# Expert stage of a streaming encoder layer: a two-slot loop on three engines becomes 32 written-out slots

## The chip, the cores and the metric

The kernel runs on one core of one Trainium2 chip. The metric is device time in microseconds from launch to end. "TensorE" multiplies matrices, "VectorE" and "ScalarE" do elementwise work, "GpSimd" and "SyncE" here mostly issue DMAs. In profile rows they are PE (PEld for its weight loads), DVE, ACT, POOL and SP; a q behind a name (SPq, PEldq) is that engine's sequencer, which issues DMAs and does register work.

## The reference

One layer of a streaming encoder for 1024 prompt tokens, 16 meta tokens and 64 sample tokens: attention and a gated recurrence side by side, then a mixture of experts, of which this is the core:

```python
gates = (one_hot(g_idx) * within * g_top).reshape(-1, N_EXPERTS)   # top group, top 2 of its 4 experts
y = zeros(t.shape)
for e in range(N_EXPERTS):                                         # 16 experts
    he = silu(t @ w1[e]) * (t @ w3[e])                             # 1024 -> 256
    y = y + gates[:, e:e + 1] * (he @ w2[e])                       # 256 -> 1024
```

Every token goes to two experts, in fp32. The 1088 tokens of the two requests give 2176 pairs of token and expert.

## The kernel before, in words

The pairs are sorted by expert and padded to tiles of 128 rows. There are at most SLOT_TILES = 32 such tiles, called slots; an expert has one or more consecutive slots. A table `expert_of`, computed on the chip, gives each slot's expert. Slot s needs the expert's first weights (w1 and w3 side by side, 2 MB), its second weights (w2, 1 MB) and 128 gathered token rows.

To keep fp32 accuracy every operand is split in a high and a low part and every product is three matmuls (L1638, L1639, L1640). The raw weights have one buffer, `w13_in`, in four chunks; they are split again for each slot, also when the expert stays the same. The work of slot s:

- SyncE (`moe_loads`): per chunk, two weight DMAs with condition `new` (L1426), which move data only if slot s has another expert than slot s-1. Before chunk c it waits until VectorE has split chunk c of slot s-1 (`s_w13lo`). Then it waits for the finished rows of slot s-3 and stores them (L1440, L1430). The order is its program's: loads of s, store of s-3, loads of s+1. It reads the expert numbers from memory into registers (L1404, L1407).
- GpSimd (`moe_pool`, written out already): gathers tokens (L1474), makes the low part of w2 (L1514) and loads w2 (L1483), with the same condition.
- ScalarE (`moe_act`): high parts of the weights of slot s+1 in four chunks (L1539), of w2 in two halves (L1559), the SiLU of slot s (L1575), the high part of the turned tokens of slot s+1 (L1547), half of the result rows of slot s-1 (L1552), the high part of the gate product (L1588).
- VectorE (`moe_dve`): the low parts of the same (L1842 weights, L1852 turned tokens, L1900 gate product), the product with the SiLU (L1889), the other half of the result rows (L1857).
- TensorE (`moe_pe`): the first product of slot s (24 matmuls of 512 columns), eight transposes of slot s+1's tokens (L1649), the second product of slot s-1 (12 matmuls), two transposes of slot s's gate rows (L1696). That is 46 matmuls and 46 weight loads a slot, in this order, on every engine's program by hand.

The four engines other than GpSimd run `body(it, j, first, last)` through `expert_turns`: slots 0 to 3 written out, slots 4 to 27 in a hardware loop of 12 turns of two slots (`eng.Fori(2, turns - 1)`), slots 28 to 31 written out. In the loop the slot number `s = it * UN + j` is in a register, so each wait such as `wait_ge(s_mh, s)` compares with a register that has to be computed first; outside it is a constant.

Of the kernel before, what the change touches and what calls it, by code (L numbers as in the profile page):

```python
# [41 lines left out]
SLOT_TILES = (2 * sum(MOE_ROWS) - NE) // P + NE  # L42
# [60 lines left out]
def hybrid_layer(nc, x_prompt, x_sample, cache_ckv, cache_krope, state_hgrn, meta_tokens, attn_norm, w_in, q_norm,  # L103
# [1269 lines left out]
    UN = 2  # L1373
# [4 lines left out]
    def uses(j):  # L1378

        return len(range(j, SLOT_TILES, UN))  # L1380

    def expert_turns(eng, body):

        turns = SLOT_TILES // UN - 1
        assert SLOT_TILES % UN == 0
        for it in range(2):
            for j in range(UN):
                body(it, j, it == 0, False)
        with eng.Fori(2, turns - 1) as it:
            for j in range(UN):  # L1390
                body(it, j, False, False)
        for it in (turns - 1, turns):
            for j in range(UN):
                body(it, j, False, it == turns and j == UN - 1)

    def is_zero(s):
        return isinstance(s, int) and s == 0

    def chunk(w, c):
        return w[:, 2 * c:2 * c + 2, :]  # L1400
# [127 lines left out]
    def moe_act(act):  # L1528
        act.wait_ge(s_rexp, 1)
        act.activation(rt[:, 8, 0:45], rt[:, 8, 0:45], ACT.Exp).then_inc(s_rexp, 1)  # L1530

        def split_weights(s, j):

            for c in range(WC):
                act.wait_ge(s_w13in[c], 32 * (s + 1))

                if c == 0 and not (isinstance(s, int) and s < UN):
                    act.wait_ge(s_mh, s - UN + 1)
                act.activation(chunk(w13_hi[j], c), chunk(w13_in, c), ACT.Copy).then_inc(s_w13hi, 1)  # L1539

        def turned(s):

            act.wait_ge(s_mx, s + 1)
            if not is_zero(s):
                act.wait_ge(s_mh, s)
            for half in range(2):
                act.activation(xg_hi[:, 4 * half:4 * half + 4, :],  # L1547
                               ps[:, half, :].rearrange("p (a b) -> p a b", a=4), ACT.Copy).then_inc(s_mxa, 1)

        def y_half(s, j):  # L1550
            act.wait_ge(s_my, s + 1)
            return act.activation(y_row[:, j, 0:512], ps[:, 6, :], ACT.Copy).then_inc(s_mya, 1)  # L1552

        def split_second(s, j, c):

            if c == 0 and not (isinstance(s, int) and s < UN):
                act.wait_ge(s_my, s - UN + 1)
            act.wait_ge(s_w2in[c], 16 * (s + 1))
            act.activation(w2_hi[j][:, c], w2_in[:, c], ACT.Copy).then_inc(s_w2hi, 1)  # L1559

        split_weights(0, 0)
        turned(0)

        def body(it, j, first, last):
            s = it * UN + j
            start = first and j == 0
            if not last:
                split_weights(s + 1, (j + 1) % UN)
            split_second(s, j, 0)
            if last:  # L1570
                split_second(s, j, 1)
            act.wait_ge(s_mh, s + 1)
            if not start:
                act.wait_ge(s_mg, s)
            act.activation(act_h, ps[:, 3 + j, 0:FF], ACT.Silu).then_inc(s_ms, 1)  # L1575
            if not last:
                turned(s + 1)
                split_second(s, j, 1)
            if not start:

                if not first:
                    free_y(act, it, j)
                y_half(s - 1, (j - 1) % UN)

            act.wait_ge(s_mgt, s + 1)
            if not start:
                act.wait_ge(s_my, s)
            act.activation(g_hi, ps[:, 2, 0:2 * P].rearrange("p (a b) -> p a b", a=2),  # L1588
                           ACT.Copy).then_inc(s_mga, 1)

        expert_turns(act, body)
        free_last(act)
        y_half(SLOT_TILES - 1, (SLOT_TILES - 1) % UN)
        for t in range(NT):
            R = MOE_ROWS[t]
            act.wait_ge(s_comb, NT + t + 1)
            if t:
                act.wait_ge(s_ysq, t)
            act.activation(y_sq[0:R], res[t][0:R, :], ACT.Square,
                           accum_out=y_stat[0:R, 0, t:t + 1]).then_inc(s_ysq, 1)  # L1600
# [17 lines left out]
    def moe_pe(pe):  # L1618

        pe.wait_ge(s_cnt, 1)  # L1620
        pe.matmul(ps[:, 0, 0:NT * NE], tab[:, C_TRI:C_TRI + P], rt[:, 15, :], start=True, stop=True)
        pe.matmul(ps[:, 1, 0:NT * NE], ones, rt[:, 15, :], start=True, stop=True).then_inc(s_rank, 1)
        pe.matmul(ps[:, 3, 0:P], ones, tab[:, C_TRI:C_TRI + P], start=True, stop=True).then_inc(s_col, 1)
        for k in range(2):
            for t in range(NT):
                n = k * NT + t
                if t == 0:
                    pe.wait_ge(s_onehot, 3 + k)
                ins = pe.matmul(ps[:, 2, 0:2 * SLOT_TILES], pos_at[0:MOE_ROWS[t], n, :], tok_at[0:MOE_ROWS[t], n, :],
                                start=n == 0, stop=n == 2 * NT - 1)  # L1630
        ins.then_inc(s_tokt, 1)
        for n in range(WARM):
            pe.matmul(ps[:, 5, :], tab[:, C_ID:C_ID + P], tab[:, C_ID:C_ID + 512], start=True, stop=True)

        def product(out, parts, w, start, stop):

            (x_hi, x_lo), (w_hi, w_lo) = parts, w
            pe.matmul(out, x_hi, w_hi, start=start, stop=False)  # L1638
            pe.matmul(out, x_hi, w_lo, start=False, stop=False)  # L1639
            return pe.matmul(out, x_lo, w_hi, start=False, stop=stop)  # L1640

        def turn(s, it, j):

            pe.wait_ge(s_xg[j], 16 * (it + 1))
            if not is_zero(s):
                pe.wait_ge(s_mxa, 2 * s)
                pe.wait_ge(s_mxv, 2 * s)
            for kc in range(KC):
                ins = pe.transpose(ps[:, kc // 4, (kc % 4) * P:(kc % 4 + 1) * P], xg[:, j, kc * P:(kc + 1) * P], ident)  # L1649
            ins.then_inc(s_mx, 1)  # L1650

        def down(s, j):

            pe.wait_ge(s_mga, s + 1)
            pe.wait_ge(s_mgv, s + 1)
            pe.wait_ge(s_w2hi, 2 * s + 2)
            pe.wait_ge(s_w2lo, 2 * s + 2)
            if not is_zero(s):
                pe.wait_ge(s_mya, s)
                pe.wait_ge(s_myv, s)  # L1660
            for n in range(2):
                cols = slice(n * 512, (n + 1) * 512)
                for c in range(2):
                    ins = product(ps[:, 6 + n, :], (g_hi[:, c, :], g_lo[:, c, :]),
                                  (w2_hi[j][:, c, cols], w2_lo[j][:, c, cols]), c == 0, c == 1)
            ins.then_inc(s_my, 1)

        pe.wait_ge(s_toki, 1)
        turn(0, 0, 0)

        def body(it, j, first, last):
            s = it * UN + j
            start = first and j == 0

            if not first:
                pe.wait_ge(s_mg, s - UN + 1)
            for kc in range(KC):
                if kc % 4 == 0:
                    pe.wait_ge(s_mxa, 2 * s + kc // 4 + 1)
                    pe.wait_ge(s_mxv, 2 * s + kc // 4 + 1)  # L1680
                if kc % 2 == 0:
                    pe.wait_ge(s_w13hi, WC * s + kc // 2 + 1)
                    pe.wait_ge(s_w13lo, WC * s + kc // 2 + 1)
                ins = product(ps[:, 3 + j, :], (xg_hi[:, kc, :], xg_lo[:, kc, :]),
                              (w13_hi[j][:, kc, :], w13_lo[j][:, kc, :]), kc == 0, kc == KC - 1)
            ins.then_inc(s_mh, 1)
            if not last:
                turn(s + 1, it + (j + 1) // UN, (j + 1) % UN)
            if not start:
                down(s - 1, (j - 1) % UN)  # L1690
            pe.wait_ge(s_mg, s + 1)
            if not start:
                pe.wait_ge(s_mga, s)
                pe.wait_ge(s_mgv, s)
            for c in range(2):
                ins = pe.transpose(ps[:, 2, c * P:(c + 1) * P], g_row[:, c * P:(c + 1) * P], ident)  # L1696
            ins.then_inc(s_mgt, 1)

        expert_turns(pe, body)
        down(SLOT_TILES - 1, (SLOT_TILES - 1) % UN)  # L1700

    def moe_dve(dve, link):
# [198 lines left out]
                              g_hi.bitcast(F32),  # L1901
                              ALU.subtract).then_inc(s_mgv, 1)

        expert_turns(dve, body)
        first_adds(range(2))
        free_last(dve)
        y_half(SLOT_TILES - 1, (SLOT_TILES - 1) % UN)
# [166 lines left out]
    def _(act):  # L2074
# [67 lines left out]
        attention_act(act)  # L2142
        end_phase(act, 1)
        moe_act(act)

    @blk.tensor
# [152 lines left out]
```

## Time and profile before

| what | value |
|---|---|
| runs before, us | 1200.32, 1204.63, 1195.77; median 1200.32 |
| profiled execution, us | 1196.12 |
| its span, first to last instruction, us | 1194.2 |
| mean granted TensorE clock | 0.962 of full |
| first product of slot 0, of slot 4, of slot 28 | 830.84, 872.40, 1109.51 us from the span's start |

Profile times count from the span's start. The profiled execution is 4.2 us below the median of the runs. Rows of a timeline read: start us, duration us, engine, line, operation, output<-input, shape, count, and in brackets the engine's idle time before and who ended it.

### The profile page before, as it was taken

Reading aid. Unit: us, or ns where it says so; the run is one execution under the profiler, and the core shown is the slowest. Engines: PE = TensorE matmul, PEld = TensorE weight load, DVE = VectorE, ACT = ScalarE, POOL = GpSimd, SP = SyncE. Lnnn points to the kernel's source line nnn. Section 1 sums busy time; section 2 is a strip of 40 time slices with the busy share of each in tenths; the row PEclk is TensorE's granted clock in tenths of the full one; section 3 lists DMA queues with packets and bytes.
Section 4 is the critical chain, followed back from the end, with each engine's and each line's share of the span. In section 5 each row is a group of like instructions: output and inputs, shape, how many; then the busy total and the mean of one; then the engine's idle time right before and its main releaser. Section 6 shows DMA issues by size and latency. Waiting matters only on the chain.

```text
span 1194.2 us, 18236 instructions
## 1 busy us (share of the span) xinstructions
PE 1065.5 (89%) x5777; PEld 860.0 (72%) x5777; DVE 697.2 (58%) x1326; ACT 525.4 (44%) x1025; POOL 344.9 (29%) x368
## 2 busy tenths in 40 slices
PE   5999999998987899999999999975999999999940
PEld 4889889984555777777778777863777777777830
DVE  4330610118666667576575655448777777787867
ACT  4432421213532333323333333313787878788823
POOL 3100510000541111111110100201656565666655
PEclk9999999999989999899999999996999999999985
DMA  7340141122579586465555444834988687877667
GB/s 273 118 164 1 45 127 64 45 78 68 195 272 364 199 322 244 174 229 207 205 198 198 156 170 151 295 143 160 302 313 325 243 282 248 284 253 255 246 240 278
DMA packets 105764, 242.83 MB, mean 203 GB/s; under 512 B 15248, under 2 KB 63840, under 8 KB 95456
## 3 DMA queue, kind: packets, MB, share of 16 engines
q1 hardware_dynamic: 81312, 117.42, 28.8%
q0 software_dynamic: 23328, 122.17, 28.7%
q10 hardware_dynamic: 1056, 2.36, 0.6%
q8 instruction: 39, 0.64, 0.2%
q14 instruction: 29, 0.24, 0.1%
HBM read 243.31 MB, written 48.94 MB: 245 GB/s over the span
## 4 chain that ended last, share of the span: by engine, by line
PE 58%; DMA 12%; DVE 9%; issue 8%; ACT 5%; SPq 5%; POOL 2%; POOLq 0%; DVEq 0%; ACTq 0%
DMA below<-in_w 8%; PE ps L1076 5%; PE ps L2189 4%; PE ps L2191 4%; PE ps L2190 4%; PE ps L929 4%; PE ps L947 3%; SPq L1426 3%; PE ps L1117 3%; PE ps L1025 3%; PE ps L1118 3%; PE ps L2184 3%; PE ps L2183 3%; PE ps L2185 3%; PE ps L1121 3%
## 5 line engine op out<-in xcount | busy, mean ns | idle before, releaser
L1842 DVE TENSOR_TENSOR low<-below,high 128x1024 fp32r<-128x1024 f32 x128 | 156.6, 1260 | 35.3 <-ACT high L1539 31.8
L1638 PE MATMUL ps<-high 128*128 128x512 f32 x384 | 156.1, 407 | 10.8 <-DVE low L1852 7.2
L1514 POOL TENSOR_TENSOR low<-below,high 128x1024 fp32r<-128x1024 f32 x62 | 129.0, 2081 | 94.0 <-ACT high L1559 93.1
L1639 PE MATMUL ps<-low,high 128*128 128x512 f32 x384 | 150.7, 392 | 0.0
L1640 PE MATMUL ps<-high,low 128*128 128x512 f32 x384 | 150.6, 392 | 0.0
L1539 ACT ACTIVATE high<-below 128x1024 fp32r<-128x1024 f32 x128 | 130.3, 1070 | 38.6 <-DMA below<-in_w 37.9
L653 ACT ACTIVATE arena<-ps 128x512 f32<-128x512 f32 (+8 forms) x100 | 50.1, 511 | 172.0 <-PE ps L929 171.6
L929 PE MATMUL ps<-arena 128*128 128x128 f32 (+4 forms) x613 | 94.3, 277 | 7.5 <-ACT arena L653 2.2
L797 POOL DMA_DIRECT2D high<-wo_dram x34 | 18.7, 549 | 281.6 <-PE ps L1121 270.8
L1638 PEld LDWEIGHTS ps<-high 128*128 128x128 f32 x384 | 72.5, 189 | 28.1 <-issue 12.8
L947 PE MATMUL ps<-arena 128*128 128x64 f32 (+2 forms) x624 | 83.4, 269 | 6.9 <-DVE arena L702 2.9
L929 PEld LDWEIGHTS ps<-arena 128*128 128x128 f32 (+4 forms) x613 | 71.4, 148 | 25.0 <-issue 17.6
L2189 PE MATMUL ps<-high 128*128 128x512 f32 (+3 forms) x216 | 83.8, 388 | 3.7 <-DVE low L2231 3.7
L947 PEld LDWEIGHTS ps<-arena 128*128 128x128 f32 (+2 forms) x624 | 77.6, 191 | 11.2 <-DVE arena L700 3.9
L896 ACT ACTIVATE arena<-ps,arena 80x320 f32<-80x320 f32 (+8 forms) x72 | 51.5, 715 | 73.9 <-DVE arena L1291 45.4
L1640 PEld LDWEIGHTS ps<-high,low 128*128 128x128 f32 x384 | 72.4, 189 | 16.0
L1076 PE MATMUL ps<-arena 96*128 96x512 f32 (+3 forms) x192 | 79.1, 522 | 5.3 <-ACT arena L902 2.8
L2041 POOL TENSOR_SCALAR arena<-arena 128x1 f32<-128x1 f32 (+7 forms) x33 | 10.3, 312 | 251.4 <-ACT arena L878 94.2
L2191 PE MATMUL ps<-high,low 128*128 128x512 f32 (+3 forms) x216 | 82.8, 383 | 0.0
L2190 PE MATMUL ps<-low,high 128*128 128x512 f32 (+3 forms) x216 | 82.6, 382 | 0.0
L1639 PEld LDWEIGHTS ps<-low,high 128*128 128x128 f32 x384 | 72.7, 189 | 13.2
L1559 ACT ACTIVATE high<-below 128x1024 fp32r<-128x1024 f32 x64 | 67.8, 1060 | 22.8 <-DMA below<-in_w 22.5
(251 smaller groups left out, 2215.8 us busy)
## 6 DMA issues: line engine op xcount, KB each, us to landing
below<-in_w SPq DMA_DIRECT2D x256, 256.0 KB
high<-wo_dram POOLq DMA_DIRECT2D x36, 1024.0 KB, 5.9
low<-wo_dram POOLq DMA_DIRECT2D x36, 1024.0 KB, 8.6
below<-in_w POOLq DMA_DIRECT2D x64, 512.0 KB
y_dram<-arena SPq DMA_DIRECT2D x32, 512.0 KB
arena<-in_x_prompt SPq DMA_DIRECT2D x15, 512.0 KB
below<-in_w_in SPq DMA_DIRECT2D x14, 512.0 KB, 7.7
out<-arena SPq DMA_DIRECT2D x9, 512.0 KB, 2.7
```

Source lines behind the costliest of these rows:

```text
L929: ins = pe.transpose(ps[0:width, 4 + g % 2, n * P:n * P + rows], src, ident[0:rows, 0:rows])
L947: ins = pe.matmul(ps[0:R, 6, hd * VD:(hd + 1) * VD], p_t[0:w, ip % 2, n, 0:R], v_rows[0:w, kb, hd * VD:(hd + 1) * VD], start=hd == 0 and g ...
L1076: ins = pe.matmul(ps[0:R, bank + n // 512, 0:m], q_t[0:QD, hd, 0:R], k_t[0:QD, hd, k0 + n:k0 + n + m], start=True, stop=True)
L1514: pool.tensor_tensor(w2_lo[s % UN][:, c], w2_in[:, c], w2_hi[s % UN][:, c].bitcast(F32), ALU.subtract).then_inc(s_w2lo, 1)
L1539: act.activation(chunk(w13_hi[j], c), chunk(w13_in, c), ACT.Copy).then_inc(s_w13hi, 1)
L1638: pe.matmul(out, x_hi, w_hi, start=start, stop=False)
L1639: pe.matmul(out, x_hi, w_lo, start=False, stop=False)
L1640: return pe.matmul(out, x_lo, w_hi, start=False, stop=stop)
L1842: dve.tensor_tensor(chunk(w13_lo[j], c), chunk(w13_in, c), chunk(w13_hi[j], c).bitcast(F32), ALU.subtract).then_inc(s_w13lo, 1)
L2189: pe.matmul(out, x_hi[:, kc, toks], wh[:, kc, 0:nn], start=kc == 0, stop=False)
L2190: pe.matmul(out, x_hi[:, kc, toks], wl[:, kc, 0:nn], start=False, stop=False)
L2191: ins = pe.matmul(out, x_lo[:, kc, toks], wh[:, kc, 0:nn], start=False, stop=kc == KC - 1)
```

## The change

The loop goes on TensorE, ScalarE and VectorE. Each calls `expert_slots`, which calls the same `body` 32 times with Python integers, so 24 slots' instructions take the place of one loop body of two. Order and number of operations stay the same, the waits get constants. SyncE still calls `expert_turns`, and GpSimd is untouched.

```diff
@@ -1379,6 +1379,11 @@
+    def expert_slots(body):
+
+        for s in range(SLOT_TILES):
+            body(s // UN, s % UN, s < UN, s == SLOT_TILES - 1)
+
     def expert_turns(eng, body):
 
         turns = SLOT_TILES // UN - 1
@@ moe_act
-        expert_turns(act, body)
+        expert_slots(body)
         free_last(act)
@@ moe_pe
-        expert_turns(pe, body)
+        expert_slots(body)
         down(SLOT_TILES - 1, (SLOT_TILES - 1) % UN)
@@ moe_dve
-        expert_turns(dve, body)
+        expert_slots(body)
         first_adds(range(2))
```

## Rows read from the trace of the kernel before

In groups 2 and 9 the columns are: stretch, its us, then busy us and (x instructions) of PE, PEld, DVE, ACT and POOL, the granted clock, the DMA engines' busy share, GB/s.

**Rows 1.** The page, part 1: busy time of each engine.

```profile
PE 1065.5 (89%) x5777; PEld 860.0 (72%) x5777; DVE 697.2 (58%) x1326; ACT 525.4 (44%) x1025; POOL 344.9 (29%) x368
```

**Rows 2.** Busy time by stretch: slots 4 to 27, then slots 28 to 31.

```profile
872.40:1109.50 237.10, 228.94 (x1104) 185.88 (x1105) 183.90 (x217) 192.65 (x265) 147.01 (x122) 1.00 0.79 277
1109.50:1147.50 38.00, 36.78 (x179) 30.24 (x177) 27.12 (x35) 28.26 (x40) 24.52 (x23) 1.00 0.54 199
```

**Rows 3.** TensorE in order of time: around the starts of slots 28, 29, 7, 16, 3.

```profile
1109.51 0.48 PE L1638 MATMUL ps<-high 128*128 128x512 f32 x1
...
1118.74 0.38 PE L1696 MATMUL ps<-arena 128*128 128x128 f32 x2
1118.87 0.48 PE L1638 MATMUL ps<-high 128*128 128x512 f32 x1
...
901.34 0.38 PE L1696 MATMUL ps<-arena 128*128 128x128 f32 x2
902.22 0.47 PE L1638 MATMUL ps<-high 128*128 128x512 f32 x1 [0.50 <-DVE low L1852]
...
991.89 0.44 PE L1696 MATMUL ps<-arena 128*128 128x128 f32 x2 [0.36 <-DVE arena L1889]
992.93 0.47 PE L1638 MATMUL ps<-high 128*128 128x512 f32 x1 [0.61 <-DVE low L1852]
...
860.24 0.38 PE L1696 MATMUL ps<-arena 128*128 128x128 f32 x2
861.07 0.47 PE L1638 MATMUL ps<-high 128*128 128x512 f32 x1 [0.46 <-ACT high L1547]
```

**Rows 4.** TensorE's waits over slots 4 to 27: total us, times, longest us.

```profile
PE ps L1638 <- DVE low L1852: 7.2, 12, 0.6
```

**Rows 5.** Line 1426 on SyncE, weight loads of slots 7 and 11: ns min/median/max.

```profile
L1426 SPq DMA_DIRECT2D below<-in_w x8: 183/396/486, 885.6 to 891.4; - x8
...
L1426 SPq DMA_DIRECT2D below<-in_w x8: 73/73/93, 926.5 to 931.9; - x8
```

**Rows 6.** ScalarE in order of time, from the split of slot 16's last chunk.

```profile
989.09 1.06 ACT L1539 ACTIVATE high<-below 128x1024 fp32r<-128x1024 f32 x1 [0.44 <-DMA below<-in_w]
990.06 1.04 ACT L1559 ACTIVATE high<-below 128x1024 fp32r<-128x1024 f32 x1
991.01 0.37 ACT L1575 ACTIVATE arena<-ps 128x256 f32<-128x256 f32 x1
991.27 1.08 ACT L1547 ACTIVATE high<-ps 128x512 fp32r<-128x512 f32 x2
```

**Rows 7.** VectorE in order of time, the same stretch.

```profile
991.89 1.29 DVE L1852 TENSOR_TENSOR low<-ps,high 128x512 fp32r<-128x512 f32 x2
993.10 0.68 DVE L1857 COPY arena<-ps 128x512 f32<-128x512 f32 x1
...
995.04 4.83 DVE L1842 TENSOR_TENSOR low<-below,high 128x1024 fp32r<-128x1024 f32 x4 [0.53 <-ACT high L1539]
```

**Rows 8.** SyncE's DMA issues in order of time, the same stretch.

```profile
994.01 0.38 SPq L1430 DMA_DIRECT2D y_dram<-arena  x1
997.34 4.96 SPq L1426 DMA_DIRECT2D below<-in_w  x8
```

**Rows 9.** Busy time, 994 to 1009: slot 18's loads (last columns: clock, DMA share, GB/s).

```profile
994.00:1009.00 15.00, 15.00 (x77) 12.57 (x76) 11.22 (x13) 11.49 (x16) 9.41 (x9) 1.00 0.93 313
```

**Rows 10.** TensorE's branch at the end of a loop turn: ns min/median/max.

```profile
L1389 PEldq COMPARE_BRANCH  x12: 76/208/230, 891.2 to 1107.3; - x12
```

**Rows 11.** Instruction queues (packets, MB, share): whole span; slots 4-27; slots 28-31.

```profile
q8 instruction: 39, 0.64, 0.2%
...
q8 instruction: 1, 0.02, 0.0%
...
q8 instruction: 2, 0.03, 0.3%
q14 instruction: 3, 0.02, 0.2%
```

## The prediction, written before the change was run

> **What bounds the kernel now.** I read the page first, then the expert stage alone, in this order: busy time by stretch, TensorE in order of time, its waits, and then ScalarE, VectorE and SyncE over one turn of the loop. The page shows TensorE busy 89% of the span [rows 1], which tells little about this stage. The stretch of the loop, slots 4 to 27, takes 237.10 us at the full granted clock [rows 2]. A slot in which nothing is late takes 9.36 us: slot 28's first product starts at 1109.51 and slot 29's at 1118.87 [rows 3]. 24 such slots would take 224.6 us, so 12.5 us of the stretch is stall. That is everything the change could win in it, and it is 1.0% of the kernel.
>
> Where does the stall stand? Between the two transposes of a slot's gate rows (L1696) and the first product of the next slot (L1638), TensorE needs 0.13 us when nothing is late (1118.74 to 1118.87). Before slot 16 it needs 1.04 us and waits for VectorE's L1852, the low part of the turned tokens [rows 3]. There are 12 such waits [rows 4]. They stand before even slots, so they could be taken for the price of the loop's branch, since a turn has two slots. They are not, and slot 7 tells the two apart: it lies in the middle of a turn, no branch stands before it, and it has the same stall, 0.88 us. What it shares with the even slots is a real weight load. SyncE issues eight weight DMAs for every slot, but when the expert is the old one their condition is false and an issue takes 73 ns in place of about 400: slot 7's are real, slot 11's are not [rows 5]. Slot 3 is the second witness. It is written out already, its waits are constants, its load is real, and it stalls too: 0.83 us between the same two instructions [rows 3]. The stalls follow the loads, not the loop.
>
> So what is the ring that paces a loaded turn? Take slot 16. ScalarE splits its last chunk of weights at 989.09, released by the DMA, and goes without a gap through the second-weight split, the SiLU and the turned tokens at 991.27 [rows 6]. VectorE follows: L1852 at 991.89, then the copy of the finished rows, 993.10 to 993.78 [rows 7]. SyncE waits for that copy, stores the rows at 994.01, and only then comes to slot 18's loads in its own order. The first is issued 3.33 us later, at 997.34, and the eight take until 1002.30 [rows 8]. VectorE's splits, which free the chunks, are done by 999.87, ahead of the last issues, so SyncE is late by its own work. The transfers then keep the DMA engines 93% busy from 994 to 1009 [rows 9], and the last chunk starts the next turn. In sum: 4.9 us on ScalarE and VectorE, 8.3 us on SyncE, and some 6.7 us from SyncE's last issue to the end of the filled stretch, 19.9 us, against 18.7 for two slots of products. TensorE is not in this ring at all, and the longest part of it is SyncE's, which keeps its loop.
>
> **The change part by part.** (1) *TensorE's branch goes.* It is there 12 times at 0.208 us [rows 10], 2.5 us in all, and it lies in the shadow of the wait for VectorE. I price it at 0; if the cover were gone it would be -2.5 us. What is late next after the branch is L1852, as now.
>
> (2) *TensorE's register arithmetic between waits goes.* The written-out slot 3 idles 0.46 us before its first product, the looped slot 16 0.61 us [rows 3]: 0.15 us per stall, 1.8 us for the 12. Only the last stall can hand this on to the end, because after each earlier one TensorE has to wait for the next load anyhow; half of a further one may come from slots that are only just late. I take -0.3 us, with bounds 0 and -1.8.
>
> (3) *Register arithmetic and branch on ScalarE and VectorE go.* In the ring their rows stand end to start (989.09, 990.06, 991.01, 991.27; 991.89 then 993.10 [rows 6, 7]): each op takes up to a microsecond and the sequencer has its arithmetic done under the one before. I take 0. The gap that the traces leave open is between the copy's end at 993.78 and SyncE's store at 994.01, and that is SyncE's own. Nothing is queued behind a new wait: order and count of waits stay, only their operands change.
>
> (4) *SyncE and GpSimd:* not one instruction changes, no DMA of the kernel moves. 0.
>
> (5) *More program to fetch.* In the loop TensorE's instruction queue moved one packet in 237 us. In slots 28 to 31 it moved two in 37.5 us, of 0.9 us each (0.3% of 16 engines), and the other engines' queue three of 0.4 us [rows 11]. Outside the loop the page has 5777 - 1104 = 4673 matmuls [rows 1, 2] on 38 packets, 123 each. The change adds 22 written slots of 46 matmuls: 1012, so 8 packets. ScalarE and VectorE have fewer instructions; I estimate 5 of their smaller packets. A packet occupies one of 16 DMA engines. It costs time only if it falls in the filled stretch (15 of about 20 us) and its engine is the last to finish the chunk. Upper bound: each adds its full time to the ring, 8 x 0.9 + 5 x 0.4 = 9.2 us; lower bound 0. I take a fifth, +1.8 us, since only one engine of many finishes last.
>
> Sum: -0.3 + 1.8 = +1.5 us, with the bounds -4.3 and +9.2. The profiled execution took 1196.12 us (span 1194.2 and 1.9 around it), so the same execution would take 1197.6. The median of the three runs before is 1200.32, 4.2 above the profiled one, and I carry the difference over: **1201.8 us**. No change is what a measurement should say; it can tell about 1% of this kernel, 12 us, from nothing.
>
> One rule speaks for a gain. On the branch itself the trace has 12 of them at 0.208 us and one TensorE packet over the whole loop [rows 10, 11]. The Trainium skill, "Runtime: NRT & Kernel Launch", section "Instruction fetch mechanics", says that a taken branch whose target is outside the current window forces a fetch of the target before execution goes on, and that kernels therefore prefer full unrolling. By that rule the loop would pay a fetch a turn; by the row it pays none, since there are no packets for it: the body stays in.
>
> **The rivals.** *A: the loop is the stall.* If register waits and the branch made TensorE late, all 12.5 us go: 1200.3 - 12.5 = 1187.8. For it: the stalls come nearly always at the turn's edge. Against: slots 7 and 3. 6%.
>
> *B: a fetch per branch.* 12 turns x 0.9 us = 10.8 us, giving 1189.5. The rule above is its page; the packet count is against it. 4%.
>
> *C: ScalarE and VectorE give the ring a little.* If some wait in the 4.9 us is released faster with a constant, say 0.3 us a loaded turn, 12 x 0.3 = 3.6 us: 1196.7. For it: slot 3's 0.15 us. Against: no gaps in rows 6. 12%.
>
> *D, the other side: fetches against weights.* All of term 5's bound is paid, where every packet meets a filled stretch and its engine finishes last; it decides from about a third of that bound on, when it outweighs C. +9.2 us: 1209.5. For it: DMA engines 93% busy just when the last chunk is due. Against: the unloaded part of each turn absorbs a packet that falls there. 10%. *D2:* in addition the fetched block itself comes late and TensorE runs dry, 8 times about 0.9 us more: 1216.7. Against: slots 0 to 3 run written out under the same load. 5%.
>
> *E: the change isn't what it says,* for instance a slot's flags differ from the loop's. The four flags agree slot by slot, so 2%, at 1200.
>
> **How the numbers follow.** My forecast holds 61%. Range: from 1191 (C, and the scatter of the runs, 4.5 us either side of the median) to 1211 (D and scatter); A, B and D2 are left out, 15%. Faster by over 1% is below 1188.3: A, 6%. Slower by over 1% is above 1212.3: D2 and a part of D, 6%. Within 1%: 88%.
>
> **What the profile after would show.** If the steps are right: the stalls before slots 6, 7, 8, 10 and every even slot to 26 are still there, waiting for L1852's successor, with about 0.46 us of idle time in place of 0.61; the stretch of slots 4 to 27 takes 235 to 241 us; SyncE still needs 3.3 us from the store of rows to the first real load and some 5 us for the eight; TensorE's instruction queue shows about 9 packets there in place of 1, and the whole program 47 in place of 39. Register instructions are gone from TensorE, ScalarE and VectorE and stay on SyncE. Wrong would be: even slots at 9.36 us with a load in flight (A), turns shorter by 0.3 us with the same SyncE times (C), or loaded turns that lengthen just when a packet is fetched (D).

## The result, and the profile after

The written-out kernel takes 1205.91 us (median of 20 runs, 1199.33 to 1212.10), the kernel before 1200.74 us beside it (20 runs, 1194.47 to 1209.55). The ratio is 1.0040, its 95% interval 1.0024 to 1.0055. So the change costs 5.2 us. That is within 1%, as forecast, but it is a real loss, more than three times the 1.5 us that the forecast's sum gave, and 4.1 us above the predicted time. In the experiments below, medians are of all runs and ratios of the undisturbed ones: one run in experiment 1, one in experiment 3 and two of the kernel before took between 1276 and 5951 us.

Line numbers of the stage are 5 higher than before (L1638 is now L1643, L1696 is L1701, L1852 is L1857, L1426 is L1431). First the page of the profile after: span, busy time, instruction queues.

```profile
span 1204.0 us, 17765 instructions
...
PE 1071.3 (89%) x5777; PEld 862.6 (72%) x5777; DVE 695.0 (58%) x1326; ACT 524.5 (44%) x1025; POOL 344.1 (29%) x368
...
q8 instruction: 48, 0.79, 0.3%
q14 instruction: 35, 0.29, 0.1%
```

TensorE's queue (q8) has 48 packets in place of 39 [rows 11]; 0.79 MB over 48 is 16 KB each. The other engines' queue (q14) has 8 KB packets. Now the stretch from slot 4's first product to slot 28's, in the columns of rows 2, and the instruction queues in it.

```profile
873.54:1119.41 245.87, 232.49 (x1105) 187.05 (x1105) 181.19 (x217) 192.58 (x265) 147.97 (x122) 0.99 0.78 268
```

```profile
q8 instruction: 10, 0.16, 0.3%
q14 instruction: 10, 0.08, 0.1%
```

In these two executions the stretch is 245.87 us against 237.10 [rows 2], 8.8 longer. That is more than the medians differ by, and one look at each kernel is not enough for it: a second look at either is told below. Ten of TensorE's packets lie in the stretch in place of one. Its waits there (total us, times, longest us) are:

```profile
PE ps L1701 <- DVE arena L1894: 6.8, 9, 1.8
PE ps L1643 <- ACT high L1552: 6.2, 13, 0.5
PE ps L1643 <- issue: 0.7, 3, 0.3
```

The stalls before the slots with a fresh load are still there, 0.48 us each (6.2 over 13) in place of 0.6 (7.2 over 12 [rows 4]); the profile now puts them down to ScalarE's high part of the turned tokens (L1552) and not, as forecast, to VectorE's low part. What has grown is the wait one instruction earlier, of the gate rows' transposes (L1701) for VectorE's gating, which is late when the loads are late: 6.8 us in all, against this row of the kernel before.

```profile
PE ps L1696 <- DVE arena L1889: 1.4, 3, 0.7
```

In the second looks told below it is 3.7 us before and 5.8 after. The waits that nothing in the profile ends ("issue") are 0.7 us, so the profile shows no long wait of TensorE for its own instructions. That is the first sign of where the time comes from: from later data.

### The profile page after: what moved, and what is told of

Same layout as the page of the kernel before. It is cut to its first block, busy times and chain, and to the rows that moved or that the text cites. A ratio compares the mean times of both kernels' runs of the same rounds, so it can differ in the third digit from the quotient of the medians.

```text
span 1204.0 us, 17765 instructions
## 1 busy us (share of the span) xinstructions
PE 1071.3 (89%) x5777; PEld 862.6 (72%) x5777; DVE 695.0 (58%) x1326; ACT 524.5 (44%) x1025; POOL 344.1 (29%) x368
## 4 chain that ended last, share of the span: by engine, by line
PE 55%; DMA 15%; DVE 9%; issue 7%; ACT 5%; SPq 5%; POOL 2%; POOLq 0%; ACTq 0%; DVEq 0%
DMA below<-in_w 8%; PE ps L1076 5%; PE ps L2194 4%; PE ps L2195 4%; PE ps L2196 4%; PE ps L929 4%; SPq L1431 3%; PE ps L947 3%; PE ps L1117 3%; PE ps L1118 3%; PE ps L2189 3%; PE ps L2188 3%; PE ps L2190 3%; PE ps L1121 3%; PE ps L1025 2%
## 5 line engine op out<-in xcount | busy, mean ns | idle before, releaser
L1643 PE MATMUL ps<-high 128*128 128x512 f32 x384 | 156.8, 408 | 10.1 <-ACT high L1552 7.7
L1643 PEld LDWEIGHTS ps<-high 128*128 128x128 f32 x384 | 72.8, 190 | 28.5 <-issue 11.4
```

## The experiments

All were timed beside the kernel before, except for two single looks. One measure recurs. *First issue to last chunk* is the time from SyncE's first real weight issue of a slot (start of the L1426 or L1431 group) to the start of ScalarE's split of that slot's last chunk. It is the part of the ring (the circle of waits that paces a *loaded turn*, two slots with one real load) in which the DMA engines are filled. One sample can be read off in full: in the profile after, slot 20 is loaded as follows (SyncE's issues, then ScalarE's splits in order of time).

```profile
1023.73 4.92 SPq L1431 DMA_DIRECT2D below<-in_w  x8
```

```profile
1030.74 1.06 ACT L1544 ACTIVATE high<-below 128x1024 fp32r<-128x1024 f32 x1 [0.80 <-DMA below<-in_w]
1032.22 1.06 ACT L1544 ACTIVATE high<-below 128x1024 fp32r<-128x1024 f32 x1 [0.42 <-DMA below<-in_w]
1034.87 1.06 ACT L1544 ACTIVATE high<-below 128x1024 fp32r<-128x1024 f32 x1 [1.58 <-DMA below<-in_w]
1036.37 1.06 ACT L1544 ACTIVATE high<-below 128x1024 fp32r<-128x1024 f32 x1 [0.44 <-DMA below<-in_w]
```

The four chunks come 1.5, 2.65 and 1.5 us apart, and the whole is 1036.37 - 1023.73 = 12.64 us. The third comes 2.65 us after the second. The DMA queues from 1031.5 to 1033.8, just ahead of it, hold this:

```profile
DMA packets 751, 0.81 MB, mean 354 GB/s; under 512 B 47, under 2 KB 725, under 8 KB 750
...
q1 hardware_dynamic: 750, 0.80, 106.3%
q8 instruction: 1, 0.02, 3.1%
```

One 16 KB packet of instructions, 3.1% of 16 engines over 2.3 us, which is 1.1 us of one engine. A gap of that size is no sign of a packet by itself. In the kernel before, slot 20 has one of 2.6 us too, but an earlier one:

```profile
1016.91 5.27 SPq L1426 DMA_DIRECT2D below<-in_w  x8
```

```profile
1022.79 1.06 ACT L1539 ACTIVATE high<-below 128x1024 fp32r<-128x1024 f32 x1
1025.39 1.06 ACT L1539 ACTIVATE high<-below 128x1024 fp32r<-128x1024 f32 x1 [1.54 <-DMA below<-in_w]
1026.91 1.06 ACT L1539 ACTIVATE high<-below 128x1024 fp32r<-128x1024 f32 x1 [0.45 <-DMA below<-in_w]
1028.39 1.06 ACT L1539 ACTIVATE high<-below 128x1024 fp32r<-128x1024 f32 x1 [0.42 <-DMA below<-in_w]
```

Counted from the first issue, the second chunk comes after 8.48 us here and 8.49 us in the written-out kernel. The third comes after 10.00 here and 11.14 there, the fourth after 11.48 and 12.64. The delay of 1.15 us stands just behind the packet. Slot 14, six slots earlier in the profile after, has no 16 KB packet:

```profile
963.23 5.43 SPq L1431 DMA_DIRECT2D below<-in_w  x8
```

```profile
971.97 1.06 ACT L1544 ACTIVATE high<-below 128x1024 fp32r<-128x1024 f32 x1 [1.17 <-DMA below<-in_w]
973.48 1.06 ACT L1544 ACTIVATE high<-below 128x1024 fp32r<-128x1024 f32 x1 [0.45 <-DMA below<-in_w]
974.97 1.06 ACT L1544 ACTIVATE high<-below 128x1024 fp32r<-128x1024 f32 x1 [0.42 <-DMA below<-in_w]
```

Here the last three chunks come 1.5 us apart, and the whole is 11.74 us, although SyncE's issues took half a microsecond longer.

**1 and 2. Which engine's writing-out costs?** Each has one half of the change: `expert_slots` for TensorE alone, or for ScalarE and VectorE alone.

```diff
-        expert_turns(pe, body)
+        expert_slots(body)
```

```diff
-        expert_turns(act, body)
+        expert_slots(body)
-        expert_turns(dve, body)
+        expert_slots(body)
```

> Only TensorE's 32 slots are written out; ScalarE and VectorE keep the loop. The changed kernel is 5.2 us slower than before (1205.91 against 1200.74). Theory F (added instruction packets share DMA engines with the weight loads and make the last chunk land later): TensorE brings 9 of the 15 added packets and all of the 16 KB ones, so about 4 us of the 5 stay, ratio 1.003, its queue shows 48 packets, and the time from SyncE's first weight issue to ScalarE's split of the last chunk is above 11.8 us on average over slots 12 to 26 (11.5 before, 12.0 after). Theory W (constants in ScalarE's and VectorE's waits shift their work against the transfers): ratio 1.000 and 11.5 us.

> Only ScalarE's and VectorE's slots are written out; TensorE keeps the loop. Theory F: 6 small packets of 8 KB more, none of 16 KB: at most 1.5 us, ratio 1.000 to 1.001, first issue to last chunk 11.5 to 11.7 us. Theory W: the whole loss, ratio 1.004, 12.0 us.

TensorE alone: 1206.31 us (1205.36 without the disturbed run) against 1200.16, ratio 1.0037 (1.0016 to 1.0057). ScalarE and VectorE alone: 1200.39 against the same 1200.16, ratio 1.0004 (0.9984 to 1.0024). The loss is that of TensorE's half. First issue to last chunk is 11.81 us on average over slots 12 to 26 with TensorE alone and 11.51 with the other two, 11.48 in the kernel before. The instruction queues in the stretch of slots 4 to 27, TensorE alone first:

```profile
q8 instruction: 10, 0.16, 0.3%
q14 instruction: 4, 0.03, 0.0%
```

```profile
q14 instruction: 10, 0.08, 0.1%
q8 instruction: 1, 0.02, 0.0%
```

So the six added 8 KB packets of the other engines cost nothing that can be measured, and the loss goes with the nine added 16 KB ones.

**3 and 4. A dose of 16 KB without the code.** The kernel before, loops kept, with one more DMA in each real load, of 16 KB or of 64 bytes, between the second and the third chunk's issues. The definitions of its two arrays and a wait for it at the end of SyncE's program are left out here.

```diff
+                if c == 2:
+                    sp.dma_start(dose_out[bass.ds(s, 1), 0:4096], dose_in[:, 0:4096], cond=new).then_inc(s_dose, 16)
                 for k in range(2):
```

Experiment 4 has `0:16` in place of `0:4096`.

> The kernel before (loops everywhere) with one extra transfer of 16 KB as a single piece from device memory to device memory, issued by SyncE between chunks 1 and 2 of each real weight load. It imitates the added packet in the worst place, in each of the loaded turns. Against x4, which has the same issue with 64 bytes: theory F expects some 0.3 to 0.7 us more per loaded turn, 4 to 9 us over the kernel. If a packet of this size costs the ring nothing: x3 equals x4 within 1.5 us.

> The control of x3: the same extra DMA issue with 64 bytes. Both theories: only SyncE's additional issue, some 0.1 to 0.5 us in each of the loaded turns, so 1 to 6 us over the kernel before, ratio 1.001 to 1.005.

16 KB: 1204.76 (1204.24 without the disturbed run), ratio 1.0034 (1.0010 to 1.0058). 64 bytes: 1202.36, ratio 1.0012 (0.9992 to 1.0032). The size accounts for 1.9 us of undisturbed medians, below what was expected, and the two intervals overlap. But the dose was not what the expectation says. The profile of experiment 3 around slot 20's load, 1024 to 1037 us, with one dose in it:

```profile
DMA packets 2817, 4.36 MB, mean 336 GB/s; under 512 B 204, under 2 KB 2268, under 8 KB 2817
...
dose_out<-in_w SPq DMA_DIRECT2D x1, 16.0 KB
```

All 2817 packets are under 8 KB, so the dose was not one packet of 16 KB. Over the whole trace there are 256 packets of 1 KB more than in the kernel before, sixteen for each of the 16 experts. An instruction packet of 16 KB was never imitated, so these two experiments say nothing of what one costs.

**5 and 6. Is SyncE the long part of the ring?** The prediction said so. Here SyncE reads a slot's expert before it waits for and stores finished rows (those of slot s-4, so as to come ahead of the loads); the first load can then follow the store at once. 5 is the kernel before with this, 6 the written-out one.

```diff
             e, new = expert(sp, s)
+            if not isinstance(s, int) or s >= 4:
+                store_y(s - 4)
+                sp.dma_start(y_dram[bass.ds((s - 4) * P, P), :], y_row[:, j, :]).then_inc(s_yst[j], 16)
...
-            if not isinstance(s, int) or s >= 3:
-                store_y(s - 3)
-                sp.dma_start(y_dram[bass.ds((s - 3) * P, P), :], y_row[:, (j + 1) % UN, :]).then_inc(
-                    s_yst[(j + 1) % UN], 16)
...
-        for s in range(SLOT_TILES - 3, SLOT_TILES):
+        for s in range(SLOT_TILES - 4, SLOT_TILES):
```

> The kernel before with one thing moved on SyncE: it reads the expert of slot s (two loads into registers and their arithmetic) before it waits for the finished rows of slot s-4 and stores them, where it did so behind the store. Nothing else changes. If the ring of a loaded turn is copy of rows, SyncE, transfers, splits, as predicted, the time from the copy to SyncE's first weight issue falls from 4.2 us to about 1.5, then VectorE's splits gate the chunks, the turns fall from 19.8 to about 18.8 us, where TensorE's products are the bound, and the kernel gains 8 to 12 us: 1189 to 1193, ratio 0.990 to 0.993. If SyncE isn't in the ring: ratio 1.000.

> The changed kernel (three engines written out) with the same move on SyncE. Theory F: the added packets cost only through the ring; with the ring about as short as the products, less than half of the 5 us between loop and written-out version is left, x6 is within 2 us of x5. If the written-out version loses somewhere else (TensorE waiting for instructions, another stage), the full 5 us stay between x5 and x6.

No gain: 1202.64 against 1201.23, ratio 1.0018 (0.9997 to 1.0038), and 1207.09, ratio 1.0044 (1.0021 to 1.0067). The two are 4.5 us apart; theory F (the added packets delay the loads) had expected less than 2. SyncE and VectorE in experiment 5, from finished rows to loads:

```profile
995.48 0.38 SPq L1417 DMA_DIRECT2D y_dram<-arena  x1
998.22 5.02 SPq L1429 DMA_DIRECT2D below<-in_w  x8
```

```profile
996.41 4.82 DVE L1841 TENSOR_TENSOR low<-below,high 128x1024 fp32r<-128x1024 f32 x4 [0.53 <-ACT high L1538]
```

The store still stands 2.7 us ahead of the loads, though the register work between them is gone. What holds the first load now is that VectorE's first split (996.41, four of 1.2 us) has to free the chunk. So copy to first issue fell only from 4.24 to 3.74 us (means over eight loaded turns), and the time from last issue to last chunk grew from 6.75 to 7.71. SyncE started half a microsecond earlier and the transfers ended no earlier: as far as that half microsecond goes, SyncE was beside the longest path and not on it.

**7 and 8. Is it the amount that is moved?** Of the second weights of slots 1 to 31, 16 of 1024 columns are fetched, so the second product of those slots multiplies with old weights; all instructions stay. 7 is the kernel before with this, 8 the written-out one.

```diff
-                pool.dma_start(w2_in[:, c], w2[0, bass.ds(e, 1), c * P:(c + 1) * P].rearrange("e p n -> p (e n)"),
+                n2 = 16 if s else D
+                pool.dma_start(w2_in[:, c, 0:n2], w2[0, bass.ds(e, 1), c * P:(c + 1) * P, 0:n2].rearrange("e p n -> p (e n)"),
```

> The kernel before, but the second weights' loads of slots 1 to 31 fetch only 16 of 1024 columns, so 1 MB less moves for each new expert; the second product then uses mostly stale weights. If a loaded turn is held by how fast the DMA engines move some 4.7 MB in it (355 GB/s before), 1 MB less is 2.7 us less, more than the 1.1 us by which the turn exceeds TensorE's 18.7: all loaded turns from slot 12 on fall to 18.7 to 18.9 us and the kernel gains 10 to 13 us, 1188 to 1191. If SyncE's own work and not the amount holds the turn, as I predicted: it stays at 19.5 or more, ratio 0.997 to 1.000.

> The changed kernel with the same cut of the second weights' loads. Theory F (packets against weights in the full DMA engines): with the engines no longer full up to the last chunk, the written-out version loses at most 1 us against x7. If the 5 us come from TensorE waiting for its own instructions or from the order of the waits: the 5 us between x7 and x8 stay.

1186.39 against 1200.82, ratio 0.9885 (0.9858 to 0.9912). The stretch of slots 4 to 27 in experiment 7:

```profile
869.00:1097.50 228.50, 226.76 (x1109) 186.79 (x1108) 182.64 (x217) 193.09 (x266) 157.59 (x122) 1.00 0.67 229
```

From slot 4's first product to slot 28's it is 228.04 us, 9.1 below before and 3.4 above the 224.6 of 24 slots without a stall. First issue to last chunk fell from 11.48 to 10.49 us and a loaded turn from 19.72 to 18.90, where two slots of products need 18.7. Nothing of the loops or of SyncE's issues was touched: the stall of the kernel before is mostly the amount of data behind a full set of DMA engines. Of the 14.4 us between the medians, the stretch holds 9.1. Experiment 8 asked whether the loss of writing out goes with it. It has 1190.93, ratio 0.9906 (0.9873 to 0.9939), 4.5 us above 7 with intervals that overlap. In the stretch the two differ by 2.8 us only (230.85 and 228.04), and 9.3 us of the 12.1 between these two profiled spans lies outside it. By the times, that neither shows nor excludes that less data removes the loss. The loads say more. Of the nine loads of slots 10 to 26 in experiment 8, three (10, 12, 20) have a 16 KB packet between first issue and last chunk and take 11.68 us on average; the other six take 10.57, and the same six take 10.55 in experiment 7. With less data the packets still delay the loads that they meet, and theory F's expectation that they would not (at most 1 us) failed.

**9 and 10. Second looks at either kernel,** because one execution of each is too little for terms of half a microsecond.

> The kernel before, unchanged, for a second profile. The first had turns of 19.72 us on average (slots 12 to 26) and 355 GB/s in the filled stretch; the changed one 20.28 us and 344 GB/s. Theory F alone: turns again 19.6 to 19.8. If the chip's rate differs from execution to execution by more than the change does, the second profile shows it: 20.0 or more.

> The changed kernel, unchanged, for a second profile beside x9. Theory F: turns in which a 16 KB packet falls between SyncE's first weight issue and the last chunk take 0.5 us or more longer than the others in the same profile, 12.4 against 11.8 us from first issue to last chunk; mean turn 20.1 to 20.4 us.

The kernel before this time took 1208.19 us and the written-out one 1204.22, the other way round from the medians. Its loaded turns took 20.07 us on average, where 19.6 to 19.8 had been expected if the chip's rate did not change; the first look had 19.72. The scatter between executions is of the size of the effect. The written-out one had 20.38. Of the 12 us between the two executions of the kernel before, 8.1 stand ahead of the stage: slot 0's first product starts at 830.84 in one and at 838.97 in the other, in code that is the same. Whole spans of single executions can't be compared here; stretches can. For slots 4 to 27 three profiles with TensorE in a loop (before, 9, 2) have 237.1, 240.7 and 241.2 us, mean 239.7; three with TensorE written out (after, 10, 1) have 245.9, 245.6 and 242.1, mean 244.5. The difference, 4.8 us, is near that of the medians; but the three of each kind lie up to 4 us apart, so it could as well be 3 or 6. Over the same six profiles, first issue to last chunk of slots 10 to 26:

| profiles | loads | mean us | s.d. |
|---|---|---|---|
| TensorE in a loop (before, 9, 2) | 27 | 11.61 | 0.32 |
| TensorE written out, no 16 KB packet in it, or one that begins in the last 0.9 us and ends later (3) | 18 | 11.87 | 0.25 |
| written out, with an earlier 16 KB packet | 9 | 12.40 | 0.32 |
| of these, packet 8 to 10.3 us after the first issue | 6 | 12.57 | |
| of these, packet 1.5 us after it | 3 | 12.07 | |

Loads with a packet are 0.53 us longer than those without, and 0.70 when it falls late; with the three borderline ones counted among those with a packet, the difference is 0.43. At the 354 GB/s shown ahead of slot 20's third chunk one of 16 engines moves 22 GB/s, so 16 KB would be 0.74 us of one engine, by estimate; the trace has the packet itself at 1.1 us.

The packets come at fixed places of the program, in slots 10, 18 and 20 each time, so it is fairer to compare a slot with itself. The most telling is slot 20: 11.48, 11.49 and 11.69 us with TensorE in a loop, 12.63, 12.82 and 12.60 with it written out, 1.13 us more on average and far outside the scatter. The turn of slots 18 and 19, which waits for this load, takes 19.71, 19.74 and 19.93 us against 20.88, 21.01 and 20.82. In the other pairs it grows as well, by 0.5 (5 and 6), 1.2 (7 and 8) and 1.5 us (11 and 12). Slot 10, with a late packet too, is 0.74 us longer, slot 18, with an early one, 0.38.

**11 and 12. Can the kernel be rid of the collision?** ScalarE splits the second weights of a slot ahead of the next slot's chunks 2 and 3, so that GpSimd and its loads start earlier; in the kernel before (11) and the written-out one (12).

```diff
...
             for c in range(WC):
+                if second and c >= 2:
+                    split_second(*second, c - 2)
                 act.wait_ge(s_w13in[c], 32 * (s + 1))
...
             if not last:
-                split_weights(s + 1, (j + 1) % UN)
-            split_second(s, j, 0)
+                split_weights(s + 1, (j + 1) % UN, (s, j))
...
             if not last:
                 turned(s + 1)
-                split_second(s, j, 1)
```

> The kernel before with ScalarE's two splits of the second weights of slot s moved ahead of chunks 2 and 3 of the weights of slot s+1, where they stood behind the last chunk. GpSimd then splits and reloads the second weights some 3 us earlier, in the stretch in which the DMA engines stand idle. If the amount in the filled stretch holds the turn, it shortens by 1 us or more to TensorE's 18.7 to 19.0 us: the kernel gains 8 to 13 us, ratio 0.989 to 0.993. If the amount does not hold it, only the 0.95 us that ScalarE has less behind the last chunk are won back per turn, with the same result or half of it; if neither, ratio 1.000.

> The changed kernel with the same move. Theory F: slack in the transfers swallows the packets: within 2 us of x11. Otherwise 5 us above x11.

Slower: 1228.05 against 1202.02, ratio 1.0229 (1.0201 to 1.0257), and 1231.65, ratio 1.0250 (1.0225 to 1.0274); the two are 3.6 us apart, where theory F had expected 2 at most. The low-part splits of VectorE and GpSimd now meet. In experiment 11, VectorE and then GpSimd:

```profile
1160.67 5.47 DVE L1843 TENSOR_TENSOR low<-below,high 128x1024 fp32r<-128x1024 f32 x2 [0.41 <-ACT high L1541]
```

```profile
1159.69 5.36 POOL L1514 TENSOR_TENSOR low<-below,high 128x1024 fp32r<-128x1024 f32 x2 [4.82 <-ACT high L1561]
```

Here two of VectorE's take 5.47 us in place of 2.4 (four took 4.83 [rows 7]), two of GpSimd's 5.36 in place of 4.1 (2 x 2.03, below). Over slots 4 to 27 of experiment 11 the groups are these, against means of 1254 ns on VectorE and 2031 on GpSimd before:

```profile
L1843 DVE TENSOR_TENSOR low<-below,high 128x1024 fp32r<-128x1024 f32 x96 | 177.9, 1885 | 23.0 <-ACT high L1541 22.9
```

```profile
L1514 POOL TENSOR_TENSOR low<-below,high 128x1024 fp32r<-128x1024 f32 x48 | 125.7, 2634 | 73.8 <-ACT high L1561 73.8
```

Even a slot without a load costs 10.6 us in place of 9.36. That the meeting is the whole of the 26 us was not shown: the order of ScalarE's splits changed too.

## Why the prediction was right or wrong

**Right: the loop costs nothing.** The stalls are where they were, in slots with a real load, and the branch and the register arithmetic gave back only the idle time that was foreseen (0.46 forecast, 0.48 measured, from 0.61). Rivals A and B fall: had the loop or a fetch per branch been the stall, experiment 1 would have gained some 11 us, and it lost 4 (ratio 1.0037). D2 falls too: TensorE did not run dry, with 0.7 us of waits of no visible cause in place of some 7. The Trainium skill, "Runtime: NRT & Kernel Launch", section "Instruction fetch mechanics", has the fetch for targets outside the current window only, and says that kernels prefer full unrolling. This loop paid no fetch, with one packet in 237 us [rows 11], and its written-out form is 0.4% slower: the preference does not hold here.

**Right, and without effect: term 2.** TensorE waits less per stall, 6.2 us in 13 waits in place of 7.2 in 12 [rows 4]. None of it is seen in the total, since the ring that delivers the weights sets the pace.

**Right: terms 3 and 4.** ScalarE's and VectorE's half is worth nothing that can be measured (experiment 2, 1.0004, 0.9984 to 1.0024).

**The step that failed: term 5's size.** The forecast as a whole held: no measurable change was foreseen to within 1%, and 1205.91 us lies in the range. But the range is wide, and the stretch of slots 4 to 27, forecast at 235 to 241 us, took 245.87, 245.6 and 242.1. The count was good (9 in the stretch and 47 in all forecast, 10 and 48 measured), and so were the bounds, 0 to +9.2. What was mis-sized is the share that is paid. I took a fifth, +1.8 us, on the reasoning that one engine of many finishes last. With the -0.3 of term 2 taken back, the measured +5.2 is 5.5 us, some 60% of the bound. The error lies in "one of many": the kernel goes on with a chunk only when both of its DMAs have counted to 16, so one late part holds it up, and a packet costs its load 1.13 us in slot 20, 0.74 in slot 10 and 0.38 in slot 18, where it falls early, and not a fifth of the 0.9 that I had priced it at. That the 16 engines are equally full, so that the one with the packet is nearly always the last, is my reading of this; the traces here do not tell the engines apart. What happened is rival D in part: its mechanism, at over half of its price, well past the third from which I let it decide. It deserved more than 10%, and its sign, a loaded turn that lengthens just when a packet is fetched, is there in slots 18 and 19.

How far does this account go? That the loss is TensorE's writing-out is shown (experiments 1 and 2). That a packet delays the load that it meets is shown by slot 20 in all pairs, and by experiment 8. The sum by packets does not close: 9 packets at 0.53 us are 4.8 us, which is the size of the loss, but only one load in three of slots 10 to 26 has its packet in the filled stretch, which gives 0.18 us per loaded turn, and the loads without a packet are 0.26 us longer than the loop's as well. That excess stands in the two profiles of the changed kernel (11.98 us), hardly in that of experiment 1 (11.65, against the loop's 11.61), whose profiled run, 1200.83 us, was one of its fastest. For it I have no cause: two executions of the same kernel differ by as much (11.48 and 11.82, means of eight), and three profiles of each form don't settle it. The pairs of loop and written-out kernel differ by 5.2 us (as timed), 4.5 (5 and 6), 4.5 (7 and 8) and 3.6 (11 and 12). Theory F had expected the last three to shrink to 2 us or less. They did not, so either less data and another order of loads do not take the packets' cost away, as experiment 8's loads say, or a part of the loss has another cause. No experiment puts a single 16 KB packet into the loop form.

One packet had a longer tail than the rest. In the profile after one of TensorE's falls at 900.4, when the first half of slot 6's second weights is due. ScalarE's split of it starts 3.46 us after the last chunk's, in place of 2.49 before, and the chain to VectorE's gating follows. TensorE in order of time, then by stretch:

```profile
905.24 0.44 PE L1701 MATMUL ps<-arena 128*128 128x128 f32 x2 [1.82 <-DVE arena L1894]
906.16 0.71 PE L1643 MATMUL ps<-high 128*128 128x512 f32 x1 [0.48 <-ACT high L1552]
906.67 0.63 PE L1644 MATMUL ps<-low,high 128*128 128x512 f32 x1
```

```profile
906.16:909.50 3.34, 3.34 (x8) 2.67 (x9) 2.32 (x4) 2.87 (x5) 2.92 (x3) 0.51 1.10 359
909.60:913.00 3.40, 3.40 (x16) 2.78 (x15) 2.66 (x3) 2.53 (x3) 2.29 (x2) 1.00 0.98 334
```

TensorE idles 1.82 us, and then the granted clock is 0.51 for some 3.4 us (the second fence, in the columns of rows 2), the lower of its two levels (1.2 GHz): 8 products in the time of 16. Slots 4 to 9 cost 64.84 us here and 60.62 before, but 64.64 in experiment 2, whose time is no worse. Such stretches of 3.4 us are in other profiles too. In slots 4 to 27 the three with TensorE in a loop have one between them, the three with it written out four, each after TensorE had idled for a late load. At half of 3.4 us lost in each, that could be up to 1.7 of the 4.8 us. Whether it is that much was not taken apart.

**Wrong, though it did not touch the sum: "the longest part of it is SyncE's".** I laid the rows of the ring end to end and called the longest one the cause. Experiment 5 took half a microsecond out of SyncE's part and the transfers gave it back; experiment 7 took data away and the stall went, from 12.5 us over the stretch to 3.4. The ring is paced mostly by the amount moved, and in such a ring I should have priced a foreign packet at what it takes from the DMA engines and not at a fifth of it.

## What to carry to other kernels

Where the DMA engines are full and an engine waits for the last part of a transfer, price a foreign packet that falls late in it at its whole time (here 0.7 to 1.1 us for 16 KB), not at a sixteenth or a fifth. A hardware loop around such a stage saves those packets, and here its branch and register waits cost nothing while data were late. Before an experiment imitates a packet by a DMA, look in the trace at the size in which it went out. Before moving the issue code of a ring, take data away once: a ring in which every part looks busy may be paced by bytes alone. Where code that was not changed scatters by 8 us between executions, compare stretches from several profiles and not spans.

## What the runs showed of the hardware that I had not expected

VectorE and GpSimd take turns when both subtract one tensor in SBUF from another. In experiment 11 the two groups together last from 1159.69 to 1166.14, 6.45 us, and the same four operations apart take 2 x 1.21 [rows 7] + 2 x 2.03 = 6.48 us, the latter from GpSimd's group in slots 4 to 27 of the kernel before:

```profile
L1514 POOL TENSOR_TENSOR low<-below,high 128x1024 fp32r<-128x1024 f32 x50 | 101.6, 2031 | 71.9 <-ACT high L1559 70.9
```

The Trainium skill, "SBUF — State Buffer", section "Who interferes with whom", has it as an exclusive lock between an operation of VectorE with two SBUF inputs and one of GpSimd that reads SBUF; the trace agrees within 0.1 us. In the kernel before the two stand one behind the other, VectorE's splits ending at 999.87 [rows 7] and GpSimd's starting after them:

```profile
1000.16 2.01 POOL L1514 TENSOR_TENSOR low<-below,high 128x1024 fp32r<-128x1024 f32 x1 [1.68 <-ACT high L1559]
```

The order that looked like waste keeps them apart: over slots 4 to 27 of the kernel before, 48 of GpSimd's 49 operations overlap one of VectorE's by 0.35 us or less.
